# A hybrid attention, mLSTM and MLP layer on one core: results taken out of PSUM ahead of the weight conversions that stand after the same half

## The reference

```
xn = rms_norm(h, norm_mix);  proj = xn @ w_in                  # q, k, v, gates of two mixers
y_fox = fox_attention(fq, fk, fv, ff)                          # 8 heads of 64, forget gates
hm    = mlstm_chunkwise(silu(causal_conv(mqk)), mv, mi, mf)    # 4 heads of 128
merged = g_fox * (y_fox @ w_up_fox) + g_ml * (y_ml @ w_up_mlstm)
h = h + merged @ w_mix_out
h = h + cross_attention(rms_norm(h), rms_norm(mem), w_xq, w_xkv, w_xo)   # 256 memory rows, 4 heads of 256
a = relu(rms_norm(h) @ w_mlp_in);  h = h + (a * a) @ w_mlp_out           # 1024 -> 4096 -> 1024
return rms_norm(h, norm_final)
```

## Time and profile before

| | |
|---|---|
| median of 3 runs | 950.41 us (949.18 to 950.52) |
| profiled execution | 950.14 us, of which span 948.4 us |
| PE busy | 936.2 us |
| DVE busy | 544.2 us |
| ACT busy | 415.6 us |
| PE clock granted, mean | 0.995 |

### The profile page before, as it was taken

How to read it: one execution, slowest core, us unless ns; L and a number is a source line. 1 busy time by engine, 2 the same in 40 slices (tenths; PEclk the granted TensorE clock), 3 DMA queues, 4 the chain that set the end, 5 groups by cost and what they waited for, 6 DMA issues and landing times.

```text
span 948.4 us, 11911 instructions
## 1 busy us (share of the span) xinstructions
PE 936.2 (99%) x4667; PEld 764.4 (81%) x4667; DVE 544.2 (57%) x942; ACT 415.6 (44%) x694; POOL 14.7 (2%) x39
## 2 busy tenths in 40 slices
PE   8999999999999999999999999999999999999997
PEld 6878777777777878889988778998888888888886
DVE  5532676343546763778333534568847866885543
ACT  5431566344423333344434533366446445634523
POOL 4000000000000000000000000000000000000000
PEclk9999999999999999999999999999999999999999
DMA  8411221122111272342521242120531261062202
GB/s 292 134 46 44 89 90 45 45 89 89 45 45 45 89 258 77 130 135 92 198 89 39 97 175 83 51 89 1 178 134 45 89 222 45 1 207 104 89 1 88
DMA packets 44815, 92.62 MB, mean 98 GB/s; under 512 B 1772, under 2 KB 1864, under 8 KB 44760
## 3 DMA queue, kind: packets, MB, share of 16 engines
q1 hardware_dynamic: 43192, 86.54, 27.1%
q0 software_dynamic: 1568, 5.32, 1.7%
HBM read 89.76 MB, written 2.10 MB: 97 GB/s over the span
## 4 chain that ended last, share of the span: by engine, by line
PE 94%; DVE 3%; ACT 1%; DMA 1%; issue 0%; SPq 0%; ACTq 0%; DVEq 0%
PE bank L1442 70%; PE bank L1473 12%; PE bank L1647 1%; PE bank L1598 1%; PE bank L1541 1%; PE bank L1568 1%; PE bank L1553 1%; PE bank L1486 1%; DVE w_lo L1046 1%; PE bank L1585 1%; PE bank L1625 1%; PE bank L1612 1%; DMA stage<-in_w_in 1%; PE bank L1586 0%; PE bank L1543 0%
## 5 line engine op out<-in xcount | busy, mean ns | idle before, releaser
L1046 DVE TENSOR_TENSOR w_lo<-stage,w_hi 128x1024 fp32r<-128x1024 f32 x174 | 205.0, 1220 | 87.5 <-ACT w_hi L763 87.1
L1442 PE MATMUL bank<-act_hi,w_hi 128*128 128x512 f32 (+1 forms) x640 | 248.3, 388 | 0.1
L1442 PE MATMUL bank<-act_hi,w_lo 128*128 128x512 f32 (+1 forms) x640 | 243.4, 380 | 0.0
L1442 PE MATMUL bank<-act_lo,w_hi 128*128 128x512 f32 (+1 forms) x640 | 243.1, 380 | 0.0
L763 ACT ACTIVATE w_hi<-stage 128x1024 fp32r<-128x1024 f32 x174 | 174.3, 1051 | 96.0 <-PE bank L1442 36.0
L1442 PEld LDWEIGHTS bank<-act_hi,w_lo 128*128 128x128 f32 x640 | 120.7, 189 | 23.3
L1442 PEld LDWEIGHTS bank<-act_hi,w_hi 128*128 128x128 f32 x640 | 121.1, 189 | 22.1 <-DVE w_lo L1046 0.6
L1442 PEld LDWEIGHTS bank<-act_lo,w_hi 128*128 128x128 f32 x640 | 121.0, 189 | 21.4
L1442 PE MATMUL bank<-w_hi,act_hi 128*128 128x512 f32 (+1 forms) x264 | 103.5, 392 | 3.2 <-DVE act_lo L1264 3.2
L1442 PE MATMUL bank<-w_hi,act_lo 128*128 128x512 f32 (+1 forms) x264 | 101.6, 385 | 0.0
L1442 PE MATMUL bank<-w_lo,act_hi 128*128 128x512 f32 (+1 forms) x264 | 101.6, 385 | 0.0
(11 more groups left out here) (276 smaller groups left out, 1261.4 us busy)
## 6 DMA issues: line engine op xcount, KB each, us to landing
stage<-in_w_in SPq DMA_DIRECT2D x20, 1024.0 KB, 5.0
stage<-in_w_mlp_in SPq DMA_DIRECT2D x16, 1024.0 KB, 5.2
stage<-in_w_mlp_out SPq DMA_DIRECT2D x16, 1024.0 KB, 5.5
stage<-in_w_xkv SPq DMA_DIRECT2D x8, 1024.0 KB, 4.9
stage<-in_w_mix_out SPq DMA_DIRECT2D x4, 1024.0 KB, 5.0
stage<-in_w_xq SPq DMA_DIRECT2D x4, 1024.0 KB, 5.1
stage<-in_w_xo SPq DMA_DIRECT2D x4, 1024.0 KB, 4.9
x_tok<-in_x SPq DMA_DIRECT2D x4, 512.0 KB, 9.7
```

The costliest lines, as they stand in the source:

```text
L1046: dve.tensor_tensor(w_lo[:, r:r + 2, :], stage_pair(pair), w_hi[:, r:r + 2, :].bitcast(F32), ALU.subtract).then_inc(s_low, 1)
L1442: ins = pe.matmul(dst, still[q], moving[q], start=(k == 0 and q == 0), stop=(k == nk - 1 and q == 2))
```

## The change

After each half the steps for the second pairs of weights (`now` and those of `soon`) are gathered in `splits`, and where the half ends a group, the group's `take` is put ahead of them. Where no group ends, the order stays.

```
-        steps += [("high_weights" if p in apart else "split_weights", p) for p in now]
-        steps += [x for x in soon if x[0] == "split_weights"]
+        splits = [("high_weights" if p in apart else "split_weights", p) for p in now]
+        splits += [x for x in soon if x[0] == "split_weights"]
         if c == UNITS[n][3] // 4 - 1 and HALF_AT[(n, j, c)] == i:
-            steps.append(("take", GROUP0[n] + j))
+            take = [("take", GROUP0[n] + j)]
+            steps += take + splits
         elif i == len(HALVES) - 3:
-            steps += [("take_first", GROUP0[n] + j), ("norm_second", 4 * NT + 1)]
+            steps += splits + [("take_first", GROUP0[n] + j), ("norm_second", 4 * NT + 1)]
+        else:
+            steps += splits
```

## The result

| | before | after |
|---|---|---|
| median | 949.79 us (948.85 to 950.52, 4 runs) | 970.44 us (968.18 to 972.27, 4 runs) |
| profiled execution | 950.14 us, span 948.4 | 972.27 us, span 970.5 |
| granted clock, mean | 0.995 | 0.991 |

The changed kernel takes 1.0215 times as long (95% interval 1.0203 to 1.0228): 20.65 us more, where the prediction had 18.65 on the profiled execution and said 969.0 us.

A forecast was written before the change was run, and what follows sets the result against it. PE was taken as the bound, busy 99% of the span, so every new wait is lost in full. Terms summed to 18.65 us on the profiled 950.14, making 968.8; with 0.3 for the median, 969.0 us, range 963.5 to 974.

The forecast's parts named there:

- Any take on ACT over 0.25 us makes PE wait: After a full half, the chain has 2.52 us and conversion takes 2.27, so a longer take ahead of it delays PE.
- x_q0: End of `x_q0` in cross-attention: conversions delay the softmax, leaving PE 2.55 us late in all after the second tile.
- restart: After a stall PE starts its second matmul 0.34 us after the first in place of 0.227, costing 0.11 us more.
- mem_v0: End of `mem_v0` in cross-attention: PE waits there for the take, so taking first gains 0.9 us.
- The pushes: Conversions delay softmax or mLSTM steps behind them: 2.55 us at `x_q0`, 2.3 at `x_q1`, 1.95 in the mLSTM.
- Direct waits only: Rival: the push through softmax, mLSTM and `up_fox` does not reach PE, so 961 us; chance 0.10.
- The clock: Rival: new waits of 1.6 to 2.3 us at eight places lower PE's clock; two drops 972 us, eight 982; chance 0.12.
- the clock stays at 1.00 through all of these: Sign expected in the changed kernel's profile: PE's granted clock stays at 1.00 through all the new waits.
- Not slower: Rival: the chain hides and only two bank waits go, giving 948.4 us; chance 0.05 together with no effect.
- The loads: SyncE's loads start up to 5 us later, put at nothing; without cover, up to 5 us more per place.

The follow-up runs named there:

- wait_only: Kernel before, order kept, but where ACT shares the take each conversion also waits for the half it stands behind; 959.38 us against 950.14, ratio 1.0109.
- relu_first: Kernel before, with only the take's relu put ahead of the conversions at the five `mlp_in` ends; 952.59 us against 950.14, ratio 1.0032.
- hidden_first: Kernel before, with the take first only at the eleven places where the prediction expected no cost; 950.3 us against 950.21, ratio 1.0008.
- gains: Kernel before, with the take first only at the ends of `up_ml0` (first group) and `mem_v0`; 948.73 us against 950.14, ratio 0.9986.
- mlp_first: Kernel before, with the take first only at the five `mlp_in` ends; 959.14 us against 950.14, ratio 1.0102.
- rest_first: Kernel before, with the take first only at the ends of `gate_fox1`, `gate_ml1` and `mix1`; 952.15 us against 950.3, ratio 1.0025.
- after_again: The changed kernel measured and profiled once more with no edit; 970.06 us against 950.3 for the kernel before, ratio 1.021.

## Why the prediction was right

**The mechanism.** "Any take on ACT over 0.25 us makes PE wait": three kernels with 0, 0.50 and 1.84 us in the way at the same places of the MLP show the chain of take, high part and low part to be the cause. The bound itself is nearer to 0.15 us: that is the spare time in wait_only, and the stalls of relu_first and of the changed kernel give 0.16 and 0.17. The 0.25 left out that DVE starts 0.03 to 0.05 us behind ACT's end, and the 0.05 us from DVE's end to PE's start, which the prediction counts only in its sum.

**The terms.** Each came within 0.15 us of its step but one, `x_q0` in the profile with the lower clock. The sets add up: 9.0 + 6.2 + 3.2 + 0.1 - 1.4 + 1.85 = 18.95 us of medians, beside 19.2 us for the whole change in profiles at full clock, and 18.65 forecast. So the places hardly act on one another. Small misses: a restart cost PE 0.13 to 0.17 us of the following half in place of 0.11, and `mem_v0` brought 0.76 for 0.9. The 1.4 us between 969.0 and the measured 970.44 is thus some 0.6 us of small misses and, for the rest, what the clock did in the runs compared.

**The pushes.** "Direct waits only" falls: at `x_q0`, `x_q1` and in the mLSTM the delay runs through maximum, exponential and scaling without loss, 2.07 us at the first tile. `wait_only` showed that at `x_q0` and `x_q1` most of it comes from the late start of the conversions and not from the take; at `gate_fox0` it is the take.

**The clock.** This rival came in part, and the sign "the clock stays at 1.00 through all of these" failed in the first profile of the changed kernel and held in the second. In the profiled execution it explains 1.2 us at `x_q0` and 1.6 in `fox_k`. The second need not come from a stall that the change adds, since hidden_first, which lost nothing anywhere, and before itself differ there by as much, and so do the two profiles of the changed program. Whether the change makes such a stretch more frequent is not shown. The forecast was for an unchanged clock, and at that the change measures 19.2 us; the medians, 20.65 and 19.76 us apart in the two comparisons, include what the clock did in their runs. Seven of the eight long waits never showed a lower clock in either profile of the changed kernel, so 982 us was far off. The Trainium skill ("TensorE: Matmul & The Clock Gate", section "HAM oscillation — how this bites in real kernels") tells of a kernel whose waits for DMA, about 3 to 5 us each, bring the slow clock back each time. No wait that the change adds is that long; the one of 1.92 us at `x_q0` was followed by the slow clock in one profile of three with that wait, and none in the MLP was. The rows from which the prediction argued are no firmer: PE waits for `act_lo` for 2.1 to 2.6 us near 8 to 11 us in all twelve profiles, and a stretch at 0.50 follows in seven of them, while in five the clock stays at 1.00.

**Not slower.** The two bank waits were real, and gains got 1.4 us for them. But they were 2 of 29 places. The advice to evacuate PSUM promptly in the Trainium skill ("PSUM — Partial Sum Buffer", section "Summary: rules for kernel authors") holds in this case where PE waits for the bank (gains); relu_first freed five banks early in that spirit and lost 2.45 us.

**The loads.** The later starts of SyncE's loads were put at nothing. The sums leave no room for more, and no wait of PE for a load is in the list. No run took that cover away by itself, so this term is not tested alone.

## What to carry to other kernels

When an engine runs a list in order, ask of each pair of neighbours which of them the bound engine needs first, and how long it has until then. Here a half lasts 2.72 us and the conversion chain takes 2.58 from the same event (720.85 to 723.43 in wait_only), so it has 0.15 us to give, while a bank is not wanted for two halves. A reorder that is right where PE waits for the bank (2 places) should be made there alone: by place it is worth 1.4 to 1.5 us, as a rule it costs 19. And work that starts early because it waits for an older event loses that start as soon as it is put behind a step that waits for a newer one.

## What the runs showed of the hardware

I had not expected the clock in `fox_k`. There the profile shows PE busy without a gap, yet the granted clock was 0.50, 1.2 GHz, for 3.4 us in before, for 6.8 us in the changed kernel, and for as long in mlp_first and rest_first:

```profile
84.00:92.00 8.00, 8.00 (x29) 6.65 (x29) 0.85 (x3) 0.00 (x0) 0.00 (x0) 0.57 0.00 0
```

(rest_first, against 1.00 in the row of hidden_first above.) In the other eight profiles it stayed at 1.00 there, after_again's among them, which is the same program as the changed kernel. "Busy" says little here, since the ends of matmuls are modelled. Ahead of the fall, in before from 81.94 to 85.09, PE runs 28 matmuls of only 12 columns, 0.11 us apart (first and last row):

```profile
81.94 1.06 PE L1518 MATMUL bank<-forget,upto 128*128 128x12 f32 x8
...
84.87 0.37 PE L1521 MATMUL bank<-forget,upto 128*128 128x12 f32 x2
```

In all four profiles the fall comes within the last 0.7 us of these 28 matmuls or 0.5 us behind them (85.51 in before). The eight others run the same 28 without a fall, so these alone do not bring it; no run took them away. A stretch of 3.4 us costs 1.6 us. The 21 runs of before beside which mlp_first was timed show such steps: ten lie from 948.5 to 949.0 us, nine from 950.1 to 950.4, two at 951.5 and 951.8. That these are runs with none, one and two such stretches fits the size. The mean granted clock of each run fits too, 0.997 in the first group, 0.995 in the other two on average, but a mean doesn't show where the clock fell. What brings a stretch on was not found, and no run was made for it. Two kernels can seem to differ by 1.6 us, 0.17%, for that reason alone; their traces, compared half by half, tell it from a true step.
